# Delta rule of the sample group: states as the moving operand, one column tile per head

## What is computed

```python
def step(S, xs):
    w_v_c, w_k_c, qk_c, q_dec_c, k_dec_c, gl = xs
    v_new = w_v_c - jnp.einsum('nhcd,nhde->nhce', w_k_c, S)
    o = jnp.einsum('nhcd,nhde->nhce', q_dec_c, S) + jnp.einsum('nhij,nhje->nhie', qk_c, v_new)
    S = S * gl[..., None, None] + jnp.einsum('nhcd,nhce->nhde', k_dec_c, v_new)
    return S, o
```

## Time and profile before

| What | us |
|---|---|
| Median of the timed runs (3) | 1233.63 |
| Lowest and highest of them | 1232.28, 1236.47 |
| Span of the profiled execution | 1228.4 |
| TensorE matmul busy in it | 1094.6 (89%) |
| VectorE, ScalarE, GpSimd busy | 387.7, 240.3, 86.3 |

### The profile page before, as it was taken

How to read it: one execution, slowest core, us unless ns; L and a number is a source line. 1 busy time by engine, 2 the same in 40 slices (tenths; PEclk the granted TensorE clock), 3 DMA queues, 4 the chain that set the end, 5 groups by cost and what they waited for, 6 DMA issues and landing times.

```text
span 1228.4 us, 15895 instructions
## 1 busy us (share of the span) xinstructions
PE 1094.6 (89%) x6152; PEld 601.8 (49%) x6152; DVE 387.7 (32%) x992; ACT 240.3 (20%) x494; POOL 86.3 (7%) x189
## 2 busy tenths in 40 slices
PE   8999988677799999998898799999999999879776
PEld 7776667364789446352333334444444634223232
DVE  2623354233683436211232120134001621123213
ACT  2320134232400113111111031131101311111102
POOL 6333130130000000000000000000000000000000
PEclk9999999898796999889989899999999998998889
DMA  9650374782700256699999994425423569999993
GB/s 296 175 174 12 99 246 134 205 338 87 267 1 1 77 154 257 283 421 421 421 421 420 419 305 152 132 78 205 146 103 138 239 249 421 423 421 420 420 420 123
DMA packets 87712, 298.75 MB, mean 243 GB/s; under 512 B 16067, under 2 KB 52475, under 8 KB 57902
## 3 DMA queue, kind: packets, MB, share of 16 engines
q1 hardware_dynamic: 73172, 273.92, 57.9%
q0 software_dynamic: 5152, 17.05, 4.6%
q10 hardware_dynamic: 9306, 6.67, 1.8%
HBM read 292.46 MB, written 5.16 MB: 242 GB/s over the span
## 4 chain that ended last, share of the span: by engine, by line
PE 76%; DMA 9%; DVE 7%; issue 3%; ACT 3%; SPq 2%; ACTq 0%; DVEq 0%
PE ps L1205 10%; PE ps L1395 9%; PE ps L760 9%; DMA arena<-in_moe_w_up 8%; PE ps L1161 5%; PE ps L1485 5%; PE ps L1232 3%; PE ps L711 3%; PE ps L720 2%; PE ps L1242 2%; PE ps L925 1%; PE ps L1388 1%; PE ps L1283 1%; PE ps L1012 1%; PE ps L991 1%
## 5 line engine op out<-in xcount | busy, mean ns | idle before, releaser
L1205 PE MATMUL ps<-arena,hT 128*32 128x512 f32 x1024 | 131.7, 658 | 23.0 <-DMA arena<-in_moe_w_up 22.4
L760 PE MATMUL ps<-hT,arena 128*128 128x288 f32 x448 | 114.1, 417 | 0.0
L1395 PE MATMUL ps<-arena,hT 128*128 128x512 f32 x256 | 112.7, 601 | 0.0
L760 PEld LDWEIGHTS ps<-hT,arena 128*128 128x128 f32 x448 | 86.5, 195 | 26.8 <-issue 1.7
L1205 PEld LDWEIGHTS ps<-arena,hT 128*32 128x32 f32 x1024 | 35.3, 119 | 106.5 <-issue 106.5
L1395 PEld LDWEIGHTS ps<-arena,hT 128*128 128x128 f32 x256 | 48.9, 192 | 60.8 <-issue 60.8
L1232 PE MATMUL ps<-arena 128*32 128x512 f32 x512 | 58.2, 595 | 3.2 <-ACT arena L1751 3.2
L1161 PE MATMUL ps<-htok,arena 128*128 128x512 f32 (+1 forms) x96 | 60.6, 765 | 0.0
L1485 PE MATMUL ps<-arena 128*128 128x512 f32 x128 | 59.2, 605 | 0.0
L2356 DVE TENSOR_TENSOR arena<-ps,lfp 128x256 f32<-128x256 f32 x16 | 6.8, 424 | 159.5 <-ACT lfp L1746 159.5
L711 PE MATMUL ps<-cum,ident 128*128 128x256 f32 x156 | 43.7, 439 | 11.8 <-issue 11.8
(11 more groups left out here) (473 smaller groups left out, 1446.1 us busy)
## 6 DMA issues: line engine op xcount, KB each, us to landing
arena<-in_moe_w_gate SPq DMA_DIRECT2D x66, 1024.0 KB, 14.5
arena<-in_moe_w_up SPq DMA_DIRECT2D x66, 1024.0 KB, 16.5
arena<-in_moe_w_down SPq DMA_DIRECT2D x66, 1024.0 KB, 21.7
arena<-in_cache_k SPq DMA_DIRECT2D x64, 256.0 KB, 3.2
arena<-in_cache_v POOLq DMA_DIRECT2D x64, 256.0 KB, 3.6
arena<-in_w_in_odd SPq DMA_DIRECT2D x16, 1024.0 KB, 10.5
arena<-in_w_in_even SPq DMA_DIRECT2D x14, 1024.0 KB, 9.3
arena<-in_w_out_odd SPq DMA_DIRECT2D x8, 1024.0 KB, 7.1
```

The lines of the kernel that those rows point to most:

```text
L760: last = mm(ps[:, c % 4, 0:T], w[:, k, P * (c % 2):P * (c % 2 + 1)], hT[:, k, :], start=k == 0, stop=k == KD - 1)
L1205: last = mm(ps[EC * j:EC * (j + 1), q % 2, :], xgT[:, k, GC * p + EC * j:GC * p + EC * (j + 1)], ring[:, sl:sl + 2, DE * k:DE * (k + 1)], ...
L1395: last = mm(ps[:, bank, :], hT[:, k, P * i:P * (i + 1)], ring[:, oslot(2 * n):oslot(2 * n) + 2, QC * k:QC * (k + 1)], start=k == 0, stop=k ...
```

## The change

The operands of `from_states` change places. For each head h, kind w (k or q) and sequence b, the stationary operand is now a [128 x 32] matrix that holds the 4 columns of sequence b in their own places and zeros elsewhere, and the moving operand is the state, 128 columns. The 8 sequences add up in PSUM, on rows 32h to 32h + 31: bank 5 for k, bank 4 for q. So each head has a column tile of its own, and the results are on (head, token) rows.

- The stationary matrices are slices of wqf (2304 columns), which GpSimd fills with zeros once the last inverse matmul is done, and into which ScalarE and VectorE then write w_k and q as before, each behind a wait for that fill.
- v_new goes to v4 and q S to q4, both [(head, token), 128]. VectorE makes v4 by four subtractions, ScalarE copies q4.
- The decayed keys of the samples go to k4 and the masked Q K^T to dq4, on (head, token) rows; dq4 takes four operations instead of one.
- `o_sample` adds q S by a matmul with a 32x32 identity and v_new by the matmul with dq4. The transposes and L2135 are gone, and ScalarE's square waits for its own copies only.
- vexp is [(head, token), sequence, 128]. `state_change` goes through the heads first, for each half of the sequences, and takes head h from rows 32h to 32h + 31.
- `from_states` is one call, between `state_step(0, 2)` and the prompt's L1023; the subtraction for the prompt's second tile comes after both.

```diff
@@ areas
+        wqf = wk(A, HB * 2 * NB * (TS + QS))
+        wqz = wqf.rearrange("p (a c) -> p a c", a=2 * HB)
+        wqd = wqf.rearrange("p (h w b c) -> p h w b c", h=HB, w=2, b=NB)
+        v4, q4 = wk(A + 2304, P), wk(A + 2432, P)
-        vexp = wk(A, NB, HB * P)
+        vexp = wk(A, NB, P)
+        k4, dq4 = wk(5632, P), wk(5760, TS)
@@ GpSimd
-            sel(bsel, [[-QS, NB]], 0, 1)
-            sel(bsel, [[QS, NB]], QS - 1, -1)
+            for h in range(HB):
+                sel(bsel[TS * h:TS * (h + 1), :], [[-QS, NB]], 0, 1)
+                sel(bsel[TS * h:TS * (h + 1), :], [[QS, NB]], QS - 1, -1)
...
+            pool.wait_ge(s.dl_t_ps, inv_no(6, 1))
+            nc.gpsimd.memset(wqf, 0.0).then_inc(s.pool_chain, 1)
@@ TensorE
-            def from_states(heads):
-                for h in heads:
+            def from_states():
+                for w in range(2):
                     for b in range(NB):
-                        last = mm(ps[:, 5, 64 * h + 8 * b:64 * h + 8 * (b + 1)], S0[:, HB * b + h, :], wq[:, h, b, :],
-                                  start=True, stop=True)
+                        for h in range(HB):
+                            last = mm(ps[TS * h:TS * (h + 1), 5 - w, 0:P], wqz[:, 2 * h + w, TS * b:TS * (b + 1)],
+                                      S0[:, HB * b + h, :], start=b == 0, stop=b == NB - 1)
                 return last
...
-            from_states((0, 1))
+            from_states().then_inc(s.dl_s_ps, 1)
             pe.wait_ge(s.dl_s, 1)
             for h in range(HB):
                 last = mm(ps[:, 3, P * h:P * (h + 1)], wkT[:, 1, h, :], Sp[:, 0, h, :], start=True, stop=True)
             last.then_inc(s.dl_s_ps, 1)
-            from_states((2, 3)).then_inc(s.dl_s_ps, 1)
-            pe.wait_ge(s.dl_s, 2)
+            pe.wait_ge(s.dl_s, 3)
             state_step(1, 2)
...
             def o_sample(h):
-                mm(ps[:, 6 + h % 2, TP:T], wv[0:TS, 2, h, :], dQK[0:TS, 2, h, 0:TS], start=False, stop=True,
-                   skip_group_check=True).then_inc(s.dl_o_ps, 1)
+                o, hs = ps[:, 6 + h % 2, TP:T], slice(TS * h, TS * (h + 1))
+                mm(o, q4[hs, :], ident[hs, hs], start=False, stop=False, skip_group_check=True)
+                mm(o, v4[hs, :], dq4[hs, :], start=False, stop=True, skip_group_check=True).then_inc(s.dl_o_ps, 1)
...
             o_prompt(0)
-            pe.wait_ge(s.dl_s, 3)
-            for h in range(HB):
-                last = tr(ps[0:TS, 4, P * h:P * (h + 1)], vsT[:, TS * h:TS * (h + 1)], ident[:, :])
-            last.then_inc(s.dl_s_ps, 1)
             o_prompt(1)
-            pe.wait_ge(s.dl_s, 4)
+            pe.wait_ge(s.dl_w, 7)
             o_sample(0)
             o_sample(1)
...
             def state_change(j):
-                h, q = j // 2, j % 2
+                q, h = j // HB, j % HB
                 if j >= 2:
                     pe.wait_ge(s.dl_su, j - 1)
-                mm(ps[:, 6 + j % 2, :], kdt[0:TS, 2, h, :], vx[0:TS, 4 * q:4 * q + 4, h, :], start=True,
+                hs = slice(TS * h, TS * (h + 1))
+                mm(ps[:, 6 + j % 2, :], k4[hs, :], vexp[hs, 4 * q:4 * q + 4, :], start=True,
                    stop=True).then_inc(s.dl_su_ps, 1)
@@ ScalarE
-                    A_(wq[:, :, :, 0:QS], src[:, :, 0:TS].rearrange("p h (b q) -> p h b q", q=QS), ACT.Copy).then_inc(s.dl_w, 1)
+                    act.wait_ge(s.pool_chain, consts_made + 3)
+                    A_(wqd[:, :, 0, :, 0:QS], src[:, :, 0:TS].rearrange("p h (b q) -> p h b q", q=QS), ACT.Copy).then_inc(s.dl_w, 1)
+            act.wait_ge(s.dl_s_ps, 2)
+            A_(q4, ps[:, 4, 0:P], ACT.Copy).then_inc(s.dl_w, 1)
...
-            act.wait_ge(s.dl_o, HB + 1)
+            act.wait_ge(s.dl_o, HB)
             A_(osq[:, :, :], oT[:, :, :], ACT.Square).then_inc(s.dl_osq, 1)
@@ VectorE
-                    V.tensor_tensor(dst[0:m, i, :, 0:m], src, dDT[0:m, i, :, 0:m], ALU.mult).then_inc(s.dl_kk, 1)
+                    if i == 2 and w:
+                        for h in range(HB):
+                            last = V.tensor_tensor(dq4[TS * h:TS * (h + 1), :], src[:, h, :], dDT[0:m, i, h, 0:m], ALU.mult)
+                        last.then_inc(s.dl_kk, 1)
+                    else:
+                        V.tensor_tensor(dst[0:m, i, :, 0:m], src, dDT[0:m, i, :, 0:m], ALU.mult).then_inc(s.dl_kk, 1)
...
-            V.tensor_tensor(wq[:, :, :, QS:2 * QS], cv[:, 0:HB, TP:T].rearrange("p h (b q) -> p h b q", q=QS),
+            dve.wait_ge(s.pool_chain, consts_made + 3)
+            V.tensor_tensor(wqd[:, :, 1, :, 0:QS], cv[:, 0:HB, TP:T].rearrange("p h (b q) -> p h b q", q=QS),
                             eR[:, 2, :, 0:TS].rearrange("p h (b q) -> p h b q", q=QS), ALU.mult).then_inc(s.dl_qdec, 1)
...
             dve.wait_ge(s.dl_s_ps, 2)
+            for h in range(HB):
+                last = V.tensor_tensor(v4[TS * h:TS * (h + 1), :], wv[0:TS, 2, h, :], ps[TS * h:TS * (h + 1), 5, 0:P],
+                                       ALU.subtract)
+            last.then_inc(s.dl_s, 1)
+            dve.wait_ge(s.dl_s_ps, 3)
             V.tensor_tensor(wv[:, 1], wv[:, 1], hv(3), ALU.subtract).then_inc(s.dl_s, 1)
-            dve.wait_ge(s.dl_s_ps, 3)
-            V.tensor_copy(vsT.rearrange("p (h b c) -> p h b c", h=HB, b=NB), sq[:, :, :, 0:QS]).then_inc(s.dl_s, 1)
...
-            dve.wait_ge(s.dl_s_ps, 5)
-            V.tensor_tensor(wv[0:TS, 2], wv[0:TS, 2], hv(4)[0:TS], ALU.subtract).then_inc(s.dl_s, 1)
-            dve.wait_ge(s.dl_s, 4)
+            dve.wait_ge(s.dl_s, 2)
             for b in range(NB):
-                V.tensor_scalar(vexp[0:TS, b, :], wv[0:TS, 2].rearrange("p h e -> p (h e)"), bsel[:, b:b + 1], None,
-                                ALU.mult).then_inc(s.dl_vexp, 1)
+                V.tensor_scalar(vexp[:, b, :], v4, bsel[:, b:b + 1], None, ALU.mult).then_inc(s.dl_vexp, 1)
...
-            V.tensor_tensor(os_, os_, sq[:, :, :, QS:2 * QS], ALU.add).then_inc(s.dl_o, 1)
-            dve.wait_ge(s.dl_o, HB + 1)
```

More of the change, by code:

```diff
@@ L102, in build @@
         lvl = sb("lvl", [P, 7, P])
-        msk = sb("msk", [TS, 5, TS])
+        msk = sb("msk", [TS, 4, TS])
+        bsel = sb("bsel", [P, NB])
         iota = sb("iota", [P, NG * GC])
@@ L122, in build @@
         same, utS, negTS, negQS = (msk[:, i, :] for i in range(4))
-        bsel = msk[:, 4, 0:NB]
         def col(i, n=1):
@@ L203, in build @@
         osr = wk(4096, T)
-        wq = wk(5632, HB, NB, 2 * QS)
+        k4, dq4 = wk(5632, P), wk(5760, TS)
         osq = wk(A + 6144, HB, T)
-        vsT = wk(A + 1536, HB * TS)
         eg = wk(A + 12704, 2, P)
@@ L625, in _ @@
             ch(nc.gpsimd.memset(msk[:, 2:4, :], 0.0))
-            ch(nc.gpsimd.memset(msk[:, 4, :], 1.0))
+            ch(nc.gpsimd.memset(bsel[:, :], 1.0))
             for m, fill in ((0, 0.0), (1, 0.0), (2, -BIG), (3, -BIG)):
@@ L1057, in broadcast @@
                    stop=True).then_inc(s.dl_oss_ps, 1)
-            vx = vexp.rearrange("p b (h e) -> p b h e", h=HB)
             def state_change(j):
-                h, q = j // 2, j % 2
+                q, h = j // HB, j % HB
                 if j >= 2:
                     pe.wait_ge(s.dl_su, j - 1)
-                mm(ps[:, 6 + j % 2, :], kdt[0:TS, 2, h, :], vx[0:TS, 4 * q:4 * q + 4, h, :], start=True,
+                hs = slice(TS * h, TS * (h + 1))
+                mm(ps[:, 6 + j % 2, :], k4[hs, :], vexp[hs, 4 * q:4 * q + 4, :], start=True,
                    stop=True).then_inc(s.dl_su_ps, 1)
@@ L1679, in _ @@
                 for h in range(HB):
-                    last = A_(kdt[0:m, i, h, :], kdt[0:m, i, h, :], ACT.Copy, scale=kdc[0:m, i, h:h + 1])
+                    last = A_(kdt[:, i, h, :] if i < 2 else k4[TS * h:TS * (h + 1), :], kdt[0:m, i, h, :], ACT.Copy,
+                              scale=kdc[0:m, i, h:h + 1])
             last.then_inc(s.dl_scaled, 1)
@@ L2109, in _ @@
                 V.tensor_copy(wv[0:m, i], hv(2 * i)[0:m]).then_inc(s.dl_w, 1)
-            sq = ps[:, 5, 0:256].rearrange("p (h b c) -> p h b c", h=HB, b=NB)
             dve.wait_ge(s.dl_s_ps, 1)
@@ L2133, in _ @@
             dve.wait_ge(s.dl_o, HB)
-            os_ = oT[:, :, TP:T].rearrange("p h (b q) -> p h b q", q=QS)
-            V.tensor_tensor(os_, os_, sq[:, :, :, QS:2 * QS], ALU.add).then_inc(s.dl_o, 1)
-            dve.wait_ge(s.dl_o, HB + 1)
             V.scalar_tensor_tensor(gT, oT, onw, gT, ALU.mult, ALU.mult)
```

## The result

| kernel | median us (lowest to highest) | profiled execution: time, span |
|---|---|---|
| before | 1235.05 (1232.28 to 1241.27), 4 runs | span 1228.4 |
| changed | 1216.51 (1212.9 to 1221.22), 4 runs | 1212.9, span 1211.3 |

The ratio is 0.9859, 95% interval 0.9817 to 0.9900: the change is faster. The forecast of 1218.6 us is a ratio of 0.9878, of the three runs known then. Measured again beside nine runs of before on one chip, it gave 0.9868 (0.9839 to 0.9897). The two measurements put the gain at 18.5 and 16.3 us, where 15.0 was forecast.

What follows compares the result with a forecast made beforehand. It took the stretch to be bound by the TensorE, VectorE and ScalarE chain, with L1012 paying for loads and half clock. 8.8 + 1.0 + 0.3 + 1.8 - 0.3 + 3.4 = 15.0 us off 1233.6 gave 1218.6 us, range 1214.5 to 1227.5.

Steps and rivals of the forecast that it cites:

- step (5): VectorE ahead of the inverse: four 32x32 operations replace one 32x128; 0.3 us lost (0.2 to 0.7).
- (1): Reads of sample states: burst 4.7, L1023 0.9, wait 0.8 us replace 15.16 us; 8.8 us gained (4.8 to 9.5).
- the load is the price: Old reads L1012, 6.63 us per burst: loading a 128x128 state to stream 8 columns sets their cost.
- (2): Second state step, L1006: 1.91 us at half clock becomes 0.9 at full; 1.0 us gained (0 to 1.0).
- (3): Outputs: 5.65 us becomes 5.3, transposes and a wait go; 0.3 us gained (1.0 gained to 0.6 lost).
- (4): Wait ahead of L1072: the square no longer waits for VectorE's q-part addition; 1.8 us gained (0 to 1.8).
- (6): GpSimd's zero fill of 2304 columns: 2.0 us, hidden, cost 0 (bounds 0 and 1.0 us).
- (7): State change L1065: neighbouring row groups overlap, a pair takes 1.05 us instead of 1.91; 3.4 us gained (lower bound 0).
- Does it last?: To the end of the span: the gain survives the DMA-bound expert weights because their stream starts earlier too.

Runs made afterwards that it cites:

- e4: Changed kernel with GpSimd's zero fill done twice in a row and both waits set behind the second; 1218.24 us, timed once.
- e6: Changed kernel with the state reads split into a k half and a q half, q behind the prompt's part; 1217.5 us, ratio 0.9866.
- e7: e6 plus head 2's outputs in PSUM bank 5 instead of bank 6; 1216.03 us (0.9848), run again 1216.68 us (0.9871).
- e3: Kernel before with 128 moving columns instead of 8 in the state reads L1012; 1223.37 us, ratio 0.9901.
- e5: Kernel before with VectorE's q-part addition (L2135) moved ahead of the vexp operations and decays; 1231.11 us, ratio 0.9988.
- e1: Changed kernel with neighbouring state changes put back on the same 32 rows; 1223.05 us, ratio 0.9896.
- e2: Changed kernel with the state reads reordered, head outside and sequence inside, so one column tile follows another; 1227.71 us, ratio 0.9929.
- e9: e7 plus two idle 256-column matmuls in the gap ahead of the first state step; 1215.28 us, ratio 0.9853.

## Why the prediction was right

From the start of the inverse to the x add, the profiled executions give 123.2 us before and 107.9 us after: 15.4 us, and 15.1 us in the second measurement. The prediction's sum was 15.0, or 15.3 without step (5), which lies ahead of the inverse. The times moved by 18.5 and 16.3 us; how much of the excess is spread between executions no run settles. That the median came within 2.1 us of the forecast (and within 0.3 in the second measurement) is partly luck: the forecast starts from a median of three runs, 1233.63 us, and the later medians of the kernel before are 1 to 1.5 us higher. Step by step:

(1) Right in size, 8.8 predicted, 9.0 from the first read to the second state step (15.22 to 6.25). The burst took 4.20 us and not 4.7: as reckoned, about 24 of its instructions ran ahead of the rise, but the trace has them start in groups of four every 213 ns, which is 53 ns each and not 60, and the others every 109 ns, 27 each and not 31.6; v4 took 1.2 us and not 0.9 (four subtractions of 0.28 us; L2065's two in 0.48 were too short a model), and the wait for VectorE ahead of the second state step 0.94 us and not 0.8. These nearly cancel, which is luck. In e4, e6 and the first profile of e7 the clock fell later, the first state step took 1.2 us and the 128 instructions 5.3, and the sum of the two was nearly the same. The prediction's "the load is the price" of the old reads was wrong: the 32 instructions of a burst took 207 ns each, and in e3 the same loads with more moving columns took 112 ns each at full clock. By its bounds it gave 4.8 us to the new shape at half clock and 4.0 to the clock. e3 changes the two in the other order and shows 5.6 to 6.4 us that need no column tiles at all, and 2.4 to 3.4 that do.

(2) Mis-sized by little: 1.0 predicted, 0.86 by the stages, 0.75 by the chain (1.91 to 1.16). By the chain the same eight take 0.89 us behind full-width matmuls (e3), 1.09 behind the reads on column tiles with no wait (e7), and 1.16 behind the wait.

(3) The sum was right, 5.3 predicted and 5.31 on the chain from 385.82 us, when the second state step ends, to L727 at 391.13 us. Its terms were not. The eight instructions of o_sample for heads 0 and 1 take 0.57 us, not 1.0, and a wait of 0.49 us for ScalarE's copy of head 0 stands behind them. The prediction had no term for it, though its shorter form stood in the earlier trace rows (0.28 us ahead of L1034). It grew for the reason that made o_sample short: heads 0 and 1 now stand on different row groups, and their instructions start in pairs 13 ns apart. Head 0 is done only when head 1 is, and nothing of head 1 is left to run while ScalarE copies head 0. Before, ScalarE's copy began 0.44 us after the first instruction of o_sample, while head 1 was still running; now it begins 0.66 us after it, behind both. e7 shows that the wait is worth 0.57 us. Heads 2 and 3 came as reckoned: 1.42 us (388.22 to 389.64), 1.45 predicted.

(4) Right: 1.8 predicted, 1.95 measured, and again 1.95 by e5, where the addition alone is moved. VectorE's vexp and decay, priced at nothing beside out_proj, did cost nothing: the last stage is the same to 0.01 us whether they start early or late.

(5) Mis-sized: the four 32x32 operations took 0.75 us, and with the 32x128 operation ahead of them 0.99 us (320.76 to 321.75):

```profile
320.96 0.75 DVE L2074 TENSOR_TENSOR arena<-ps,arena 32x32 f32<-32x32 f32 x4
```

Before, one 32x128 operation stood in their place and both of L2065 took 0.48 us; with one of them unchanged the pair now takes 0.99. This is 0.5 us lost, where 0.3 (0.2 to 0.7) was predicted. The first inverse matmul starts 0.5 us earlier all the same, since the clock happened to be high from 318.1 to 321.5 us in the profile of the changed kernel. That is not a property of the change.

(6) Right: 2.02 us, predicted 2.0 from two smaller fills, hidden; e4 shows that another 2 us would be too.

(7) Right: 1.06 us a pair, 1.05 predicted, 3.41 us in all, 3.4 predicted. The bound taken was a row of column tiles, and it held for row groups; e1 makes it certain that the neighbours matter. 1.91 to 1.06 is 1.8 times. The Trainium skill's page "TensorE: Matmul & The Clock Gate", Part 3, has 3.07 times for four row tiles; what two give here agrees with the prediction's estimate from it, nearly twice.

Does it last? Yes. From the x add to the end of the span it is 779.4 us before and 777.4 to 779.8 in the kernels with the change. That does not mean that no transfer is waited for. The chain of the changed kernel has three waits for layer 0's expert weights, where the earlier trace rows was the longer of two:

```profile
505.74 21.01 DMA arena<-in_moe_w_up
...
572.97 20.97 DMA arena<-in_moe_w_up
...
634.71 18.89 DMA arena<-in_moe_w_up
```

60.9 us of waiting in place of 35.2, yet from the x add to the last matmuls of the experts (L1263, before L1260) it is 275.1 us against 274.0. My reading, which no experiment tests: this stage has its length from the stream of weights, and how much of it the chain books as waiting says nothing of a loss, as long as the stream starts earlier too. The 1.2 us more here are made up by a stretch of low clock in layer 1 that before had and the changed kernel had not (1.7 us in the gated MLP), and by 0.7 us in its experts. The span's 17.1 us are thus 15.4 between the inverse and the x add, 0.5 of the start, and 1.2 behind the x add that differ from execution to execution.

## What to carry to other kernels

Before making matmuls smaller, read the granted clock beside them: here a burst of 128x128 loads with 8 moving columns ran at half clock although TensorE was busy throughout, the same burst with 128 was faster, and with two idle matmuls in a gap the clock did not fall in the one execution profiled. If small loads are wanted, let neighbouring instructions change the column tile or the row group; the same instructions tile by tile lost 7.6 of the 8.8 us of the first stage. And for each wait that a change removes, ask for the next one: here it was a PSUM bank, whose smaller wait stood in the rows of before.

## What the runs showed that I had not expected

- The clock. With 8 moving columns on 128x128 loads TensorE stayed at half clock through two bursts and more, from about 376.3 to 396.8 us, busy all the time from the first state step on. The other kernel with 8 moving columns (e5) did the same, from 378.6 to 399.1 us. With 128 moving columns in the same instructions (e3) it was at 1.00 again by 385 us, inside the first burst; and it came back as well when only one 32-column tile was used at a time (e2, 1.00 from 389.5 us on).
- With two idle matmuls (1.06 us) in a gap of 0.77 us it stayed at 1.00 through the state step, the reads and the outputs (e9, one profile).
- At a change of column tile four instructions of the next tile start beside the last four of the old one: sixteen in 1.34 us in place of sixteen times 109 ns (e2).
- Eight matmul instructions of full width take 0.2 us more right behind matmuls on column tiles than behind others: by the chain 1.09 against 0.89 us in one profile at full clock (e9, L1031 and the first L1013).
- The start of the inverse moves between 325.2 and 334.0 us over the 13 profiled executions, about half of the gain measured here, and two executions of the same kernel differ by 4.8 us (325.2 and 330.0, changed).
